# Delta rule: the transposed update is turned from a copy, and the two heads of a pair run half a level apart

## The reference

```python
a_low = jnp.where(strict, bc[..., :, None] * kk * decay_mat, 0.0)
rhs = jnp.concatenate([vc * bc[..., None], kc * (bc * jnp.exp(gcum))[..., None]], -1)
sol = lax.linalg.triangular_solve(jnp.eye(CHUNK) + a_low, rhs, left_side=True, lower=True, unit_diagonal=True)
u, w = sol[..., :dv], sol[..., dv:]
def step(s_st, chunk):
    uc, wc, ac, qec, kdc, gec = chunk
    v_new = uc - jnp.einsum('bhld,bhdv->bhlv', wc, s_st)
    o = jnp.einsum('bhld,bhdv->bhlv', qec, s_st) + jnp.einsum('bhij,bhjv->bhiv', ac, v_new)
    return s_st * gec[..., None, None] + jnp.einsum('bhld,bhlv->bhdv', kdc, v_new), o
```

## Time and profile before

| | us |
|---|---|
| three runs | 4101.89, 4104.45, 4107.82 (median 4104.45) |
| the profiled execution | 4099.06, of which its span is 4097.2 |
| delta stage of the first layer of the second block | 1935 to 2178 of the span |
| delta stage of the second layer | 3248 to 3489 |
| PE busy over the span | 3783.7 (92%) |
| DVE, ACT, POOL busy | 1854.9 (45%), 1196.2 (29%), 175.8 (4%) |

### The profile page before, as it was taken

How to read it: one execution, slowest core, us unless ns; L and a number is a source line. 1 busy time by engine, 2 the same in 40 slices (tenths; PEclk the granted TensorE clock), 3 DMA queues, 4 the chain that set the end, 5 groups by cost and what they waited for, 6 DMA issues and landing times. The chain is left out here.

```text
span 4097.2 us, 51286 instructions
## 1 busy us (share of the span) xinstructions
PE 3783.7 (92%) x20561; PEld 3123.6 (76%) x20561; DVE 1854.9 (45%) x2503; ACT 1196.2 (29%) x1767; POOL 175.8 (4%) x214
## 2 busy tenths in 40 slices
PE   6877999989999978999999989998899999998997
PEld 6755999985788856876887868876686688777885
DVE  3365534325544234356555443333435664454333
ACT  2144312215322134223223232214423222323222
POOL 0000000000000000000330000000000033000000
PEclk9888999988999989999999999999999999999998
DMA  2100222211222220221002222221122100222222
GB/s 107 47 22 21 93 89 86 83 64 28 90 95 94 91 77 22 102 83 62 1 1 78 93 72 87 103 77 63 42 84 91 52 1 1 98 72 92 98 86 84
DMA packets 49634, 279.93 MB, mean 68 GB/s; under 512 B 10453, under 2 KB 13533, under 8 KB 20197
## 3 DMA queue, kind: packets, MB, share of 16 engines
q1 hardware_dynamic: 49434, 277.13, 19.3%
HBM read 274.80 MB, written 2.27 MB: 68 GB/s over the span
## 5 line engine op out<-in xcount | busy, mean ns | idle before, releaser
L334 PE MATMUL ps<-xs,ffn_w 128*128 128x512 f32 x2112 | 483.4, 392 | 29.5 <-DVE xs L599 29.5
L334 PEld LDWEIGHTS ps<-xs,ffn_w 128*128 128x128 f32 x2112 | 399.2, 189 | 114.2 <-issue 31.1
L334 PE MATMUL ps<-u,mlp_w 128*128 128x264 f32 (+1 forms) x2880 | 456.2, 321 | 14.8 <-DVE mlp_w L593 10.0
L334 PEld LDWEIGHTS ps<-u,mlp_w 128*128 128x128 f32 x2880 | 417.3, 190 | 53.3 <-issue 15.5
L334 PE MATMUL ps<-hn,mlp_w 128*128 128x264 f32 (+1 forms) x2304 | 363.7, 320 | 0.0
L334 PEld LDWEIGHTS ps<-hn,mlp_w 128*128 128x128 f32 x2304 | 332.5, 188 | 30.3 <-issue 0.5
L334 PE MATMUL ps<-xs,cv_w 128*128 128x512 f32 x1152 | 278.1, 402 | 8.6 <-DVE cv_w L593 8.6
L334 PEld LDWEIGHTS ps<-xs,cv_w 128*128 128x128 f32 x1152 | 218.5, 191 | 75.0 <-issue 23.2
L334 PE MATMUL ps<-ff,ffn_w 128*128 128x512 f32 x1056 | 240.0, 389 | 0.0
L381 ACT CAST ffn_w<-raw 128x2048 fp32r<-128x2048 f32 (+1 forms) x74 | 124.0, 1676 | 383.2 <-PE ps L334 343.2
L334 PEld LDWEIGHTS ps<-ff,ffn_w 128*128 128x128 f32 x1056 | 198.3, 188 | 41.1
(11 more groups left out here) (413 smaller groups left out, 5334.3 us busy)
## 6 DMA issues: line engine op xcount, KB each, us to landing
raw<-in_w_ffn_up SPq DMA_DIRECT2D x44, 1024.0 KB, 4.7
raw<-in_w_up SPq DMA_DIRECT2D x32, 1024.0 KB, 4.7
raw<-in_w_down SPq DMA_DIRECT2D x32, 1024.0 KB, 4.8
raw<-in_w_conv SPq DMA_DIRECT2D x24, 1024.0 KB, 4.7
raw<-in_w_ffn_down SPq DMA_DIRECT2D x32, 704.0 KB, 4.0
raw<-in_w_mqk SPq DMA_DIRECT2D x10, 1024.0 KB, 4.8
raw<-in_w_mv SPq DMA_DIRECT2D x8, 1024.0 KB, 4.7
raw<-in_w_mo SPq DMA_DIRECT2D x8, 1024.0 KB, 4.8
```

The costliest lines, as they stand in the source:

```text
L334: ins = nc.tensor.matmul(bank(u)[:, h, :], w[:, s, wp, k * g.bw + j * P:k * g.bw + (j + 1) * P], g.xs[:, xp, k, h * n:(h + 1) * n], start= ...
```

## The change

z is no longer a product. ScalarE also copies w from PSUM to a new tile `w` in SBUF (`w_copied`), and TensorE turns that copy with four transposes into bank 1. VectorE's u update in levels 1 to 5 waits for that copy too, because the next w overwrites the bank. And head 1 of a pair runs half a level behind head 0: TensorE's order in a level is now y of head 0, w of head 1 of the level before, w of head 0, z of head 1 of the level before, prepare head 0, z of head 0, y of head 1, prepare head 1. After level 6 there is a w of head 1 by itself. The other engines' orders follow that.

```diff
-            f = {name: sb(name) for name in ("t", "y", "nb")}
+            f = {name: sb(name) for name in ("t", "y", "nb", "w")}
...
+                def y_of(i, b, e, f, s):
+                    pe.wait_ge(s["nb_done"], levels * i + b + 1)
+                    pe.wait_ge(s["t_done"], (levels - 1) * i + b)
+                    each(e, 0, f["nb"], f["t"], s["y_filled"])
+
+                def w_of(i, b, e, f, s):
+                    pe.wait_ge(s["y_copied"], (levels - 1) * i + b)
+                    pe.wait_ge(s["u_done"], levels * i + b)
+                    each(e, 2, f["y"], f["u"], s["w_filled"])
+
+                def z_of(i, b, e, f, s):
+                    pe.wait_ge(s["w_copied"], (levels - 2) * i + b)
+                    turn(e, 1, f["w"], s["z_filled"])
...
+                    for e, f, s in both:
+                        pe.wait_ge(s["nb_done"], levels * i + 1)
+                        if i:
+                            pe.wait_ge(s["nwt_done"], i)
+                        turn(e, 0, f["nb"], s["y_filled"])
+                    if i:
                         for e, f, s in both:
-                            pe.wait_ge(s["nb_done"], levels * i + b + 1)
...
+                            pick_squares(i - 1, e, f, s)
+                    if i + 1 < pairs:
+                        for e, f, s in both:
+                            prepare(i + 1, 0, e, f, s)
+                    for b in range(1, levels):
+                        y_of(i, b, *both[0])
+                        if b > 1:
+                            w_of(i, b - 1, *both[1])
+                        w_of(i, b, *both[0])
+                        if b > 1:
+                            z_of(i, b - 1, *both[1])
                         if i + 1 < pairs:
                             prepare(i + 1, b, *both[0])
-                        if b:
-                            for e, f, s in both:
-                                pe.wait_ge(s["y_copied"], (levels - 1) * i + b)
-                                pe.wait_ge(s["u_done"], levels * i + b)
-                                each(e, 2, f["y"], f["u"], s["w_filled"])
-                                if b < levels - 1:
-                                    each(e, 1, f["u"], f["y"], s["z_filled"])
+                        if b < levels - 1:
+                            z_of(i, b, *both[0])
+                        y_of(i, b, *both[1])
                         if i + 1 < pairs:
                             prepare(i + 1, b, *both[1])
+                    w_of(i, levels - 1, *both[1])
...
                     for b in range(1, levels):
-                        for e, f, s in both:
-                            act.wait_ge(s["y_filled"], levels * i + b + 1)
-                            nc.scalar.copy(f["y"][:, :, :], bank(e, 0)).then_inc(s["y_copied"], 1)
-                        if i + 1 < pairs and b in (2, 3):
-                            decays(i + 1, *both[b - 2])
+                        copy_y(i, b, *both[0])
+                        if b > 1:
+                            copy_w(i, b - 1, *both[1])
+                        if b < levels - 1:
+                            copy_w(i, b, *both[0])
+                        if i + 1 < pairs and b == 3:
+                            decays(i + 1, *both[1])
+                        copy_y(i, b, *both[1])
+                        if i + 1 < pairs and b == 2:
+                            decays(i + 1, *both[0])
...
+                def take_w(i, b, e, f, s):
+                    dve.wait_ge(s["w_filled"], (levels - 1) * i + b)
+                    if b < levels - 1:
+                        dve.wait_ge(s["w_copied"], (levels - 2) * i + b)
+                    nc.vector.tensor_tensor(f["u"][:, :, :], f["u"][:, :, :], bank(e, 2), ALU.subtract).then_inc(s["u_done"], 1)
+
+                def take_z(i, b, e, f, s):
+                    dve.wait_ge(s["z_filled"], (levels - 2) * i + b)
+                    nc.vector.tensor_tensor(f["t"][:, :, :], f["t"][:, :, :], bank(e, 1), ALU.subtract).then_inc(s["t_done"], 1)
...
                     for b in range(1, levels):
+                        if b > 1:
+                            take_w(i, b - 1, *both[1])
+                        take_w(i, b, *both[0])
+                        if b > 1:
+                            take_z(i, b - 1, *both[1])
                         if i + 1 < pairs:
                             prepared(i + 1, b, *both[0])
-                        for e, f, s in both:
-                            dve.wait_ge(s["w_filled"], (levels - 1) * i + b)
-                            if b < levels - 1:
-                                dve.wait_ge(s["z_filled"], (levels - 2) * i + b)
-                                nc.vector.tensor_tensor(f["t"][:, :, :], f["t"][:, :, :], bank(e, 1), ALU.subtract).then_inc(s["t_done"], 1)
-                            nc.vector.tensor_tensor(f["u"][:, :, :], f["u"][:, :, :], bank(e, 2), ALU.subtract).then_inc(s["u_done"], 1)
+                        if b < levels - 1:
+                            take_z(i, b, *both[0])
                         if i + 1 < pairs:
                             prepared(i + 1, b, *both[1])
+                    take_w(i, levels - 1, *both[1])
```

More of the change, by code:

```diff
@@ L2216, in delta_rule @@
         names = ("spread khat_done kb_done arg_done dm_done eg_done kk_done n_done qk_done att_done qe_done turned_k kd_done kbe_done "
-                 "turned_v vb_done nb_done y_filled y_copied z_filled w_filled t_done u_done w_turned nwt_done "
+                 "turned_v vb_done nb_done y_filled y_copied z_filled w_filled w_copied t_done u_done w_turned nwt_done "
                  "vn_filled vn_copied o_filled o_copied squared picked s_filled s_done").split()
@@ L2307, in _ @@
                 for i in range(pairs):
-                    for b in range(levels):
-                        for e, f, s in both:
-                            pe.wait_ge(s["nb_done"], levels * i + b + 1)
[L2311 to L2318, removed]
-                            for e, f, s in both:
-                                pick_squares(i - 1, e, f, s)
+                    for e, f, s in both:
[3 more added lines that the diff above has]
+                        turn(e, 0, f["nb"], s["y_filled"])
@@ L2371, in decays, with copy_y, copy_w @@
                     ins.then_inc(s["dm_done"], 1)
+                def copy_y(i, b, e, f, s):
+                    act.wait_ge(s["y_filled"], levels * i + b + 1)
+                    nc.scalar.copy(f["y"][:, :, :], bank(e, 0)).then_inc(s["y_copied"], 1)
+                def copy_w(i, b, e, f, s):
+                    act.wait_ge(s["w_filled"], (levels - 1) * i + b)
+                    nc.scalar.copy(f["w"][:, :, :], bank(e, 2)).then_inc(s["w_copied"], 1)
                 for e, f, s in both:
```

## The result

| | us |
|---|---|
| before, 4 runs | 4103.17 (4098.41 to 4107.82) |
| after, 4 runs | 4134.77 (4132.62 to 4135.14) |
| ratio | 1.0076, 95% interval 1.0059 to 1.0093 |
| profiled execution after | 4135.14, span 4133.3 (before 4099.06, span 4097.2) |

What follows compares the result with a forecast made beforehand. TensorE's issue bound the kernel before; a loop of waits was to bind it after. Six pairs at +1.8 (+10.8) and two last pairs at +4.7 (+9.4) give +20: 4119 profiled, 4124.5 as median, range 4092 to 4146.

Steps and rivals of the forecast that it cites:

- the likeliest case: The forecast itself, whole kernel: +8 to +30 us against before, chance 0.55, with its own range of 4113 to 4135.
- The levels: Levels 2 to 5 with preparation: a loop of waits sets the pace, 28.03 us where before took 27.59, +0.44 a pair.
- Rival 1: Levels with preparation: TensorE binds, not the loop; -12 us, 4092, chance 0.13; with the ends covered too 4069, chance 0.05.
- The end of a pair: From y of head 0 in level 6 to the second w_turned: +3.25 us with preparation, +3.55 without, not covered.
- The last pair: Each of the two last pairs: -0.35 in level 1, +1.47 in four levels, +3.55 at the end, +4.7 us.
- Turning z: TensorE, delta stages: four transposes replace each of 80 z blocks, at most 80 x 0.45 = 36 us less.
- The start of a pair: Level 1 of each of six pairs with preparation, priced mostly at half clock: 1.9 us less.
- rival 3's mild form: Level 1's low clock lasts 3.4 us longer, +1.7 in six pairs: 4135; chance 0.13 for both clock forms together.
- a spread: A step on TensorE, priced at 0.66 us at full clock; level 2, which holds it, was walked to 6.67.
- the exponentials in level 3: Head 0's exponentials, put behind head 1's y copy in level 2, delay the next y copy: level 3 about +0.64 us.
- Rival 3's heavy form: The last pairs' clock falls too, a level there about 9.9 instead of 6.0: +40, some 4170; chance 0.13 for both forms.
- The waiting copy: VectorE's u update waits for ScalarE's copy of w in each level; the hand-over was taken as 0.08 us.

Runs made afterwards that it cites:

- the in-step kernel: The changed kernel with both heads in step instead of half a level apart, z still turned from the copy of w: 4071.47 us, ratio 0.9921 against before.

## Why the prediction was right, and which term was mis-sized

The direction was right, and 4134.77 lies in the range of 4092 to 4146 and at the upper edge of the likeliest case's (4113 to 4135), 10 above the forecast of 4124.5. By its steps:

- **The levels.** Levels 4 and 5 were walked to 6.90 and 6.92 and measured 6.93 and 6.91, level 3 to 7.54 and measured 7.28, a level of the last pair 6.01 and 6.01. That the loop and not TensorE sets them is shown by three runs: an edit of VectorE's order shortens them, an edit of ScalarE's copy lengthens them nearly one for one, and without the stagger the levels 3 and 4 fall to TensorE's work (6.28). Rival 1 is out.
- **The end of a pair.** Forecast 8.59, measured 8.61 and 8.65. The half level that head 1 owes is its cause: with the stagger and no copies of w it is there too (7.85), and without the stagger it is gone (5.39). Six times 3.3 and twice 3.6 us, it is the largest loss.
- **The last pair.** Forecast +4.7; it takes 37.87 for 33.19, +4.7. Only its level 1 was 0.07 shorter.
- **Turning z.** "It is the most that the change can give", 36 us: the in-step kernel is 33.9 under the before that ran beside it (4105.41), some 9 of it by the clock. The prediction said that the gain is spent in waits; this shows that it is there to be had.
- **The start of a pair is the term that was mis-sized.** The prediction took 1.9 off each of six pairs in level 1 and 0.4 off level 2: 99.3 us of before for the levels 1 and 2 of six pairs should have become 85.5. They became 96.0, 10.5 more, 3.9 of it in level 1 and 6.6 in level 2. Three things were left out. First, all six level 1 of before were priced as at the low clock, from two rows; two of the six were not (7.86 and 7.05 against 10.23). And the new level 1 was walked to 8.3 in pair 1 with y of head 0 still at the full clock's pace; it took 9.6, with the low clock from y on, so that w starts 2.55 after y and not 1.84:

```profile
2016.90 1.58 PEld L2257 LDWEIGHTS ps<-delta_t,delta_nb 128*128 128x128 f32 x8 [0.37 <-issue]
2019.45 1.78 PEld L2257 LDWEIGHTS ps<-gates_w,delta_y 128*128 128x128 f32 x8 [0.97 <-ACT delta_y L2391]
```

Second, after's low clock lasted into level 2 in three pairs of six (8.4 to 8.9 where the others took 6.9), 5.4 together, as in the rows of pair 1 in the section on the result. A longer low clock is rival 3's mild form, which the prediction priced at 1.7 in each of six pairs, 4135 in all; that this is the measured time to 0.3 us is in part luck, since other terms had their share. Third, a spread was priced at 0.66, from its start to the next block. Before's own level 2 (7.07 for six blocks of 0.893 and two spreads) makes it 0.86, and level 2 at the full clock came to 6.87 and not 6.67, 1.2 in six pairs. With the exponentials in level 3 0.25 cheaper six times (-1.5), the sum of 20.1 becomes 29.1, and the stages show 29.3. The clock is also why the stages grew unevenly where 10 was forecast for each: before had it low in all three level 1 with preparation of the first stage and in one of the second, after in two of each.
- **Rival 3's heavy form** didn't happen: the last pair's levels kept a granted clock of 1.00 (24.06 us window), with 74% of a level filled when the transposes count and 59% without them, as the prediction counts it. The Trainium skill ("TensorE: Matmul & The Clock Gate", Part 4: PE-mode transpose) says that transposes don't count toward the clock. The clock held in this stage, so the stage neither bears that out nor speaks against it.
- **The waiting copy.** The prediction took the hand-over from ScalarE to VectorE as 0.08; it is 0.11. Why VectorE waits for w's copy was told too narrowly: the copy and the u update both read the bank of w. The Trainium skill ("PSUM — Partial Sum Buffer", in its table of terms) says that two engines may not use the same bank at once, reads against reads included. No run here shows it, and leaving out that wait was not tried.

**Open.** Which pair gets the low clock, and when, is not explained. Products in the thin places remove it in most pairs of after and before and not in all, and in the in-step kernel they moved it. Outside the stages 5.3 of the profile's 36 us lie ahead of the first stage. That is within the scatter of the execution: the in-step kernel, profiled twice, begins that stage at 1952.0 and at 1958.0, and the kernels with the same code ahead of it begin it between 1950.6 and 1962.8. Where that scatter comes from wasn't looked at.

## What to carry to other kernels

Replacing work of the busiest engine by a copy on an idle one puts the copy's whole hand-over (here about 1.8 us from block to block) into the dependence: walk one period with the distances between starts, every engine's order included, and compare it with the busy engine's work. In this kernel, staggering two chains cost the stagger at every place where both must be done; with only six levels between such places that was 2.5 to 3.6 us each time, and it covered almost nothing that the in-step order left open. Try the cheap order of the helping engine first: moving one VectorE operation gave back 16 us, and keeping the heads in step made the same turned z 0.8% faster than before and 1.5% faster than the change as it stood.

## What the hardware showed that I had not expected

- Sums of start distances from a few rows of the kernel before gave the period of an order that had never run, to 0.02 us in the levels 4 and 5, the levels of the last pair and the end of a pair with preparation (0.07 in the last pair's end). They missed level 2 by 0.2 and level 3 by 0.26.
- Throwaway products, four in the first level of every pair and six more behind the squares, brought the time down by 12.6 us: level 1 is 5.8 where the clock stayed at 1.00, and some 9.6 at the low clock in after.
- Before spans 4092.26 to 4111.05 over 23 runs, and 9.4 us over the 4 beside after, while after spans only 2.5 over its 4. Between before's level 1 of 10.23 and of 7.05, in pairs 1 and 2, lies only the granted clock (0.67 and 1.00), 3.2 us a pair, so where the clock falls could make a scatter of that size; that it does was not shown.
